# Expert down projection: both halves as three rounded products, with one buffer of twice the size for the rounded weights

## What is computed

```
def _hier_moe(xn, w_group, b_group, w_erouter, b_erouter, w_exp_gate, w_exp_up, w_exp_down):
    ...
    for e in range(N_EXPERTS):
        he = jax.nn.silu(xf @ w_exp_gate[e]) * (xf @ w_exp_up[e])
        y = y + combine[:, e:e + 1] * (he @ w_exp_down[e])
```

## Time and profile before

| | us |
|---|---|
| median of 3 runs | 718.75 (718.56 to 719.70) |
| the profiled execution | 719.03 |
| its span, first to last instruction | 717.2 |
| stretch of the expert loop on PE | some 399 to 687 |

### The profile page before, as it was taken

The page is one execution under the profiler, slowest core; times in us unless marked ns, Lnnn a source line. Parts: engine busy times, 40 slices in busy tenths (PEclk is TensorE's granted clock), DMA queues, the critical chain, the costliest instruction groups (busy, mean ns, idle before and its releaser), DMA issues.

```text
span 717.2 us, 8212 instructions
## 1 busy us (share of the span) xinstructions
PE 634.5 (88%) x2972; PEld 478.1 (67%) x2972; DVE 549.2 (77%) x757; ACT 374.3 (52%) x524; POOL 135.9 (19%) x102
## 2 busy tenths in 40 slices
PE   5999999896693969999998899999999999999920
PEld 5677777674693968997788566666666666666610
DVE  2179887899899999874569688888787887778506
ACT  2120113651831422744348487777788888888422
POOL 1019870243494620040000000000000000000030
PEclk8799999998697989999989999999999999999975
DMA  9766063324033231514071799999999999997144
GB/s 267 225 196 235 1 235 118 116 83 152 1 118 118 109 126 52 194 23 176 1 287 65 270 344 388 405 402 402 390 413 405 390 413 393 401 403 295 45 152 131
DMA packets 46069, 160.29 MB, mean 223 GB/s; under 512 B 7574, under 2 KB 10886, under 8 KB 33718
## 3 DMA queue, kind: packets, MB, share of 16 engines
q1 hardware_dynamic: 39232, 154.13, 56.8%
q10 hardware_dynamic: 6086, 3.06, 2.0%
q0 software_dynamic: 704, 2.49, 1.1%
HBM read 145.51 MB, written 15.02 MB: 224 GB/s over the span
## 4 chain that ended last, share of the span: by engine, by line
PE 55%; DVE 4%; ACT 2%; issue 1%; DMA 1%; POOL 0%; POOLq 0%; DVEq 0%; ACTq 0%
PE bank L1615 25%; PE bank L1640 14%; PE bank L1434 7%; PE bank L1529 5%; PE bank L1577 1%; DMA ring<-expert_rows,row_i 1%; ACT hi_gu L807 1%; PE bank L1501 1%; PE bank L1627 1%; DVE x L1351 1%; DVE conv L1069 1%; DVE gel_lo L1027 0%; PE bank L1491 0%; DVE x L1365 0%; POOL ring L542 0%
## 5 line engine op out<-in xcount | busy, mean ns | idle before, releaser
L1270 DVE TENSOR_TENSOR lo_gu<-ring,hi_gu 128x2048 fp32r<-128x2048 f32 x64 | 143.8, 2289 | 36.7 <-ACT hi_gu L807 36.6
L1439 PE MATMUL bank<-work,ring 128*128 128x304 f32 x512 | 135.7, 426 | 1.0 <-ACT work L589 1.0
L959 DVE SCALAR_TENSOR_TENSOR work<-work,par 128x272 f32<-128x272 f32 x240 | 131.8, 622 | 0.0
L1439 PEld LDWEIGHTS bank<-work,ring 128*128 128x128 f32 x512 | 99.2, 194 | 35.8 <-issue 3.1
L807 ACT ACTIVATE hi_gu<-ring 128x2048 fp32r<-128x2048 f32 x64 | 118.5, 1900 | 0.0
L1615 PE MATMUL bank<-hi_gu,xe_hi 128*96 128x512 f32 x256 | 102.9, 402 | 2.3 <-issue 2.3
L1615 PE MATMUL bank<-lo_gu,xe_hi 128*96 128x512 f32 x256 | 101.3, 396 | 0.0
L1615 PE MATMUL bank<-hi_gu,xe_lo 128*96 128x512 f32 x256 | 100.6, 393 | 0.0
L542 POOL DMA_INDIRECT ring<-expert_rows,row_i x6 | 5.7, 953 | 323.4 <-DMA expert_rows<-outst 321.9
L1640 PE MATMUL bank<-ring,windows 128*96 128x512 f32 x128 | 65.3, 592 | 0.0
L1434 PE MATMUL bank<-xn_hi,w_hi 128*128 128x304 f32 x128 | 41.1, 321 | 26.0 <-DVE xn_lo L1027 13.5
(11 more groups left out here) (279 smaller groups left out, 1156.7 us busy)
## 6 DMA issues: line engine op xcount, KB each, us to landing
ring<-w_exp_gate SPq DMA_DIRECT2D x32, 1024.0 KB, 7.1
ring<-w_exp_up SPq DMA_DIRECT2D x32, 1024.0 KB, 9.5
ring<-w_exp_down SPq DMA_DIRECT2D x32, 1024.0 KB, 9.3
ring<-w_in SPq DMA_DIRECT2D x11, 2048.0 KB, 8.9
expert_rows<-outst SPq DMA_DIRECT2D x32, 384.0 KB, 7.3
ring<-w_rnn_proj SPq DMA_DIRECT2D x2, 2048.0 KB, 7.8
ring<-w_conv_proj SPq DMA_DIRECT2D x2, 2048.0 KB, 8.4
ring<-w_out SPq DMA_DIRECT2D x2, 2048.0 KB, 8.1
```

The costliest lines, as they stand in the source:

```text
L959: ins = vec.scalar_tensor_tensor(y, glu[:, ch, w:w + TP], pcw[:, w, ch:ch + 1], y, ALU.mult, ALU.add)
L1270: vec.tensor_tensor(part, whole, as_f32(high), ALU.subtract).then_inc(out_done, 1)
L1439: ins = mm(bank[m % 4][:, 0:T], mix_w[b % MIX_SLOTS][:, i, (c % MB) * P:(c % MB + 1) * P], xnT[:, i], start=(i == 0), stop=(i == KT - 1))
```

## The change

The second half of the down weights is split as the first: ACT makes two rounded copies for each expert, DVE two subtractions, and PE runs twelve rounded matmuls in place of six rounded and two plain ones. `hi_dn` is no longer two buffers of one half, used by experts in turn, but one buffer for both halves, in the same memory. It can be written only when the down product of the expert before has been read out of it, and so `split_down(e)` moves: from the end of turn e-1 of the loop to turn e, on ACT behind `results(e-1)`, on DVE behind `hT_lo(e)`, and on both ahead of the window of e+2. `hT_hi` and `hT_lo` are 192 columns wide, and `hT_f` is gone.

```
-        hi_dn = [rounded(f"hi_dn{b}", "work", at_hi + 2 * GU_WORDS + b * D, D) for b in range(2)]
+        hi_dn = rounded("hi_dn", "work", at_hi + 2 * GU_WORDS, FT * D).rearrange("p (j n) -> p j n", j=FT)
...
-                    nc.scalar.activation(hi_dn[e % 2], w_dn[s][:, 0], ACT.Copy).then_inc(ehi_dn, 1)
+                    if e:
+                        act.wait_ge(dn_mm, r * NE + e)
+                    for j in range(FT):
+                        nc.scalar.activation(hi_dn[:, j], w_dn[s][:, j], ACT.Copy).then_inc(ehi_dn, 1)
...
-                    nc.scalar.activation(hT_hi, bank[2][:, 0:C], ACT.Copy)
-                    nc.scalar.activation(hT_f, bank[2][:, C:2 * C], ACT.Copy).then_inc(hT_act, 1)
+                    nc.scalar.activation(hT_hi, bank[2][:, 0:FT * C], ACT.Copy).then_inc(hT_act, 1)
                     if e:
                         results(e - 1)
+                        split_down(e)
                     if e + 2 < NE:
                         window(e + 2, first_token(e + 2))
-                    if e + 1 < NE:
-                        split_down(e + 1)
...
-                    split(lo_dn[s], w_dn[s][:, 0], hi_dn[e % 2], ehi_dn, r * NE + (e + 1), elo_dn)
+                    for j in range(FT):
+                        split(lo_dn[s][:, j], w_dn[s][:, j], hi_dn[:, j], ehi_dn, r * (FT * NE) + (FT * e + j + 1), elo_dn)
...
-                    vec.tensor_tensor(hT_lo, bank[2][:, 0:C], as_f32(hT_hi), ALU.subtract).then_inc(hT_dve, 1)
+                    vec.tensor_tensor(hT_lo, bank[2][:, 0:FT * C], as_f32(hT_hi), ALU.subtract).then_inc(hT_dve, 1)
+                    if e:
+                        split_down(e)
                     if e + 2 < NE:
                         window(e + 2)
-                    if e + 1 < NE:
-                        split_down(e + 1)
...
-                    pe.wait_ge(elo_dn, r * NE + (e + 1))
+                    pe.wait_ge(elo_dn, r * (FT * NE) + (FT * e + FT))
...
-                        for j, (hp, w) in enumerate(((hT_hi, hi_dn[b]), (hT_lo, hi_dn[b]), (hT_hi, lo_dn[s]), (hT_f, w_dn[s][:, 1]))):
-                            ins = mm(bank[4 + n][0:C], hp, w[:, at], start=(j == 0), stop=(j == 3))
+                        for j in range(FT):
+                            tok = slice(j * C, (j + 1) * C)
+                            for i, (hp, w) in enumerate(((hT_hi, hi_dn), (hT_lo, hi_dn), (hT_hi, lo_dn[s]))):
+                                ins = mm(bank[4 + n][0:C], hp[:, tok], w[:, j, at],
+                                         start=(i == 0 and j == 0), stop=(i == 2 and j == FT - 1))
```

More of the change, by code:

```diff
@@ L192, in trunk @@
         w_dn = [w.rearrange("p (j n) -> p j n", j=FT) for w in w_dn_flat]
-        lo_dn = [rounded(f"lo_dn{s}", "ring", e0[s] + 2 * KT * F, D) for s in range(EXP_SLOTS)]
+        lo_dn = [rounded(f"lo_dn{s}", "ring", e0[s] + 2 * KT * F, FT * D).rearrange("p (j n) -> p j n", j=FT) for s in range(EXP_SLOTS)]
         halves = rounded("halves", "ring", e0[EXP_SLOTS - 1], 2 * 2 * NT * 512)\
@@ L222, in trunk @@
         iota = win[:, 0:SLOTS]
-        hT_hi, hT_lo = (rounded(f"hT_{n}", "windows", SLOTS + i * C, C) for i, n in enumerate(("hi", "lo")))
-        hT_f = win[:, SLOTS + 2 * C:SLOTS + 3 * C]
+        hT_hi, hT_lo = (rounded(f"hT_{n}", "windows", SLOTS + i * FT * C, FT * C) for i, n in enumerate(("hi", "lo")))
         outst = sb("outst", 9 * P)
```

## The result

The changed kernel takes 735.87 us (median of 4 runs, 734.04 to 738.62) against 719.23 us (718.56 to 721.48) before: a ratio of 1.0225 with a 95% interval from 1.0190 to 1.0261. It is slower, well clear of the spread of the runs; whether by more than 2% the interval leaves open. The forecast was 729.9 us in a range of 726 to 736; the way is right and the time lies just inside the upper end, but it moved by some 16.5 us where 11.1 were worked out.

A forecast was written before the change was run, and what follows sets the result against it. The loop was taken to be bound by a circle over two experts through PE, ACT and DVE. Head 1.06 + 0.1, loop 7.2 and end 2.76 gave 11.1 us on 718.75: 729.9 us, range 726 to 736 (own range 727 to 735).

The forecast's parts named there:

- The circle's own uncertainty: In the loop, hT_lo, PE's start and the turn's load were uncertain: 17.96 to 18.5 us for two experts.
- a mild row store: Part of the row-store rival that the 726 to 736 us range was said to hold besides the forecast's own range.
- the row store: Rival: results, store issue and landing close their own circle in the loop, 9.7 us a turn, 748 us; chance 0.08.
- The circle over two experts: Loop: 8.48 us of PE plus 9.68 over ACT and DVE, 18.16 for two experts, 9.08 a turn against 8.82.
- PE's own leg: PE's part of the loop's circle: down product, turn, gate and up of e+2, 8.48 us, then +0.20 to the silu.
- Two of the signs: Loop: PE idle about 1.2 us every second expert or 0.6 at each; DVE waits 1.3 us for hi_gu in most turns.
- costed ACT at nothing: Loop: ACT's hi_dn copies end before their lo_dn, so no cost unless results come over 0.2 us later than the turn read.
- The gap at the end: Ahead of expert 31's down product nothing covers the split: 5.34 us where it was 1.90, 3.44 us more.
- the clock rival: Rival: each 1.2 us loop stall puts PE's matmuls at 0.43 us apart, 15 times, 24 us, giving 754 us; chance 0.03.
- The head: Ahead of the loop: ACT's whole first copy shows, 1.06 us, plus hT_lo of expert 0, 0.1 us.
- my own sign, 0.9 us: Head counts as wrong if the first gate and up product starts less than 0.9 us later.
- The rival that PE sets the pace: Rival: PE still paces the loop, 30 turns at -0.34 us, with head and end -6.3, 712.5 us; chance 0.06.

The follow-up runs named there:

- the run with head and end covered: Changed kernel with a third half buffer, expert 0's down weights split behind the gather, expert 31's second half at the end of turn 30: 713.33 us against 720.35, ratio 0.9916.
- three half buffers: Changed kernel with a third half buffer, so only the second half of e is split at the change's place: ratio 1.0016 to the kernel before.
- the one with three half buffers and ACT's store: Changed kernel with a third half buffer taken in turn and the row store issued by ACT on its own DMA queue: ratio 0.9996 to the kernel before.

## Why the prediction was right, and where it was short

**The mechanism was right; that the time lies inside the range is in part luck.** The circle's own uncertainty gave 727 to 735 us, and 735.87 is above that. The last microsecond of the range, put on for a mild row store, holds it, and two of the four executions (736.33 and 738.62) are above 736. Two costs that the sum left out, the row store and the slow product at the end, are partly balanced by a cost at the head that this execution did not show.

**The circle over two experts was right, and 0.2 us short.** 18.16 us were worked out, 18.36 measured. From the silu to the end of the second `lo_dn` it was exact: 534.25 - 524.91 = 9.34 us, against 9.54 - 0.20. Short was PE's start behind that wait, taken as 0.14 us from the end of the earlier trace rows: the second `lo_dn` ends at 534.25 and the matmul starts at 534.51, 0.26 us, and it is so in every such row above (0.25 us of issue). Short also was PE's own leg, from the down product to the silu: 543.28 - 534.51 = 8.77 us against 8.48 + 0.20, of which the turn without a stall has 0.03 (8.51 us) and the first matmul behind a stall some 0.05. 29 turns of 0.1 us more are 2.9 us.

Two of the signs came out otherwise. PE's idle time ahead of the down product alternates (0.77 and at most 0.2 us where the store does not disturb it) in place of 1.2 us at every second expert, and so does DVE's wait for `hi_gu` (1.27 and 0.49 us; 20.2 us in 26 waits), which was to stay at 1.3 us in most turns. Over two experts PE stands still 18.36 - 2 x 8.51 = 1.34 us, near the 1.2; how it is shared between them was not foreseen.

**The row store was not the bound, but it was not free.** Its rival's mechanism is there, with a price of at most 1.8 us instead of 18. The step that failed is my argument against it, that with 3% more time the queue would shorten. From 440 to 640 the DMA moved 402 GB/s before and 383 after, and the landing of a row store went up, from 7.4 to 7.9 us, not down (before, then changed):

```profile
expert_rows<-outst SPq DMA_DIRECT2D x22, 384.0 KB, 7.4
```

```profile
expert_rows<-outst SPq DMA_DIRECT2D x21, 384.0 KB, 7.9
```

Why a store lands no sooner when less is asked for is open. ACT's wait for it did not grow (13.0 us in 16 waits before, 13.2 in 19 after); what is new is that the down product now stands behind that wait. I had costed ACT at nothing unless the results came over 0.2 us later than in the one turn that I read, where they start 4.78 us after the silu. In the changed kernel they start more than 4.98 us after it in 8 of 31 turns, and `lo_dn` ends up to 1.0 us late for it. The trace of the kernel before could have priced that: there, too, the results pass 4.98 us, in 9 of 31 turns. One turn was read where the spread of all of them was wanted.

**The gap at the end was right** (3.09 against 3.1 us). What I left out is that PE is idle for 4.9 us there, and that the clock rival, which I had tied to stalls of 1.2 us in the loop, applies to this gap. The down product took 4.81 instead of some 3 us, 1.8 us more. In the loop, after stalls of up to 1.3 us, the product takes 3.0 us and the granted clock stays at 1.00 (last section), so the rival in the form in which I put it is refuted.

**The head was right as a wait, and hidden by chance in this execution.** The line that answers to the earlier trace rows has PE idle 1.74 us for ACT instead of 0.80, 0.94 us more against 1.06. But in this execution the router ahead of it was done 0.66 us sooner (ACT's first `hi_gu` copy starts at 376.12, against 376.78 before). So the first gate and up product starts only 0.27 us later (399.70 against 399.43): by my own sign, 0.9 us, the head would be wrong, and with the router's 0.66 it is 0.93. That product also ran for a shorter time at half clock, so that down(0) is where it was. In the seven other runs that split expert 0's down weights at the same place, down(0) lies later, at 414.33 to 419.40.

**The sum.** 2.9 us from the circle's legs, up to 1.8 from the row store, 1.5 at the last down product and -1.1 at the head are 5.1 of the 5.4 us between 11.1 and 16.5. The rival that PE sets the pace had 0.34 us a turn to gain; nearly all of that gain is real (8.51 us for PE's own turn against 8.82, and 713 us in the run with head and end covered). It was lost not to the products, but to having both `lo_dn` on the circle: with one there the loop keeps PE's pace, in the kernel before (8.84 us) as with three half buffers (8.62).

## What to carry to other kernels

When work of a helper engine is moved nearer to its user, write down the circle it then closes: from the user's start, through everything that is queued ahead of the helper's work, back to the user's start some turns later, divided by the turns. An engine that idles 20% of its time gives no help where its idle time lies ahead of the queue and the work behind it. And one buffer of twice the size is not two buffers: the memory is the same, but the distance between writing and reading is a turn shorter; a third buffer of half the size brought the turn below what it was before. And read the spread of a wait over all turns before calling it harmless, not one turn.

## What the hardware showed that I had not expected

The share of time in which the DMA engines are busy was 1.00 or 1.01 at 384, at 405 and at 413 GB/s (540 to 640 in the changed kernel, the kernel before, and the one with three half buffers and ACT's store). So a share of 1.00 did not mean that no more could be moved. The three lines, in that order (the last three columns are granted clock, DMA share, GB/s):

```profile
540.00:640.00 100.00, 94.47 (x414) 64.61 (x413) 90.06 (x77) 87.31 (x99) 0.00 (x0) 1.00 1.00 384
```

```profile
540.00:640.00 100.00, 100.00 (x410) 65.14 (x409) 81.68 (x68) 80.95 (x105) 0.00 (x0) 1.00 1.00 405
```

```profile
540.00:640.00 100.00, 100.00 (x442) 69.26 (x441) 96.43 (x83) 93.22 (x106) 0.00 (x0) 1.00 1.01 413
```
